# A hybrid decoder layer with a routed mixture of experts: expert work in units of 32 token rows instead of 64, on quarters of the TensorE array

## What is computed

```python
g_idx = jnp.argmax(group_logits, axis=-1)
e_logits = jnp.take_along_axis(all_logits, g_idx[:, None, None], axis=1)[:, 0]
top_vals, top_loc = lax.top_k(e_logits, TOP_K)                 # TOP_K = 2
expert_ids = g_idx[:, None] * EXPERTS_PER_GROUP + top_loc
...
def expert_block(args):
    xb, e = args                                               # w1, w3: [1024, 512], w2: [512, 1024]
    return (jax.nn.silu(xb @ w1[e]) * (xb @ w3[e])) @ w2[e]
```

```
32 30 35 4 19 24 25 81 | 7 33 82 50 39 34 26 15 | 25 60 105 78 45 57 23 91 | 7 57 41 63 48 38 51 75
59 24 17 36 35 77 26 130 | 12 9 11 5 13 4 12 12 | 18 19 7 17 16 23 9 9 | 0 8 4 1 3 6 14 12
```

## Time and profile before

| | |
|---|---|
| median of 3 runs | 2536.66 us |
| the profiled execution, its own time | 2528.26 us |
| its span on the core | 2526.5 us |
| first matmul of the first unit, end of the last one's | 1382.65 us, 2457.95 us |
| PE busy, DMA read from HBM | 1996.8 us (79%), 481.17 MB |

### The profile page before, as it was taken

One profiled execution on the slowest core, in us unless ns is written; L12 is line 12 of the kernel. 1 busy time (PEld: TensorE's weight loads), 2 busy tenths in 40 slices (PEclk: granted clock), 3 DMA queues, 4 the chain that ended last, 5 costly groups with the idle time before them and its releaser, 6 DMA issues.

```text
span 2526.5 us, 23324 instructions
## 1 busy us (share of the span) xinstructions
PE 1996.8 (79%) x7526; PEld 921.6 (36%) x7527; DVE 477.5 (19%) x919; ACT 272.2 (11%) x488; POOL 211.3 (8%) x318
## 2 busy tenths in 40 slices
PE   6345789689899999998971888888888888878770
PEld 5235544554444444443540232332323323222220
DVE  3534210420211111111233111101111011100005
ACT  3000210212000000000110000110010010100002
POOL 1480000000000000000003000000101000000002
PEclk9765699889899999999985999999999999998995
DMA  7020312000011111103132999999999989999985
GB/s 255 0 63 3 125 42 63 25 0 25 34 38 37 37 37 37 37 33 138 67 154 96 377 401 396 406 411 393 380 410 387 403 338 405 402 406 407 412 331 199
DMA packets 144850, 518.79 MB, mean 205 GB/s; under 512 B 29376, under 2 KB 66272, under 8 KB 127904
## 3 DMA queue, kind: packets, MB, share of 16 engines
q1 hardware_dynamic: 121952, 456.39, 47.0%
q0 software_dynamic: 9888, 38.08, 4.4%
q10 hardware_dynamic: 12976, 23.87, 2.6%
HBM read 481.17 MB, written 35.95 MB: 205 GB/s over the span
## 4 chain that ended last, share of the span: by engine, by line
PE 71%; DVE 11%; DMA 8%; POOL 3%; ACT 3%; issue 3%; SPq 1%; POOLq 0%; ACTq 0%; DVEq 0%
PE act_bank L656 22%; PE act_bank L911 18%; PE dve_bank L656 15%; PE act_bank L926 8%; DMA unit<-in_w 7%; DVE unit L1147 2%; DVE gain_a L1531 2%; PE dve_bank L903 2%; PE dve_bank L663 1%; SPq L441 1%; PE dve_bank L733 1%; PE dve_bank L809 1%; DVE rows_store L1536 1%; DVE gain_a L1534 1%; ACT gain_a L1084 1%
## 5 line engine op out<-in xcount | busy, mean ns | idle before, releaser
L656 PE MATMUL act_bank<-norm_store,unit 128*128 128x512 f32 x896 | 394.4, 594 | 8.7 <-DVE unit L1388 8.7
L911 PE MATMUL act_bank<-unit,gain_a 128*64 128x512 f32 x1504 | 345.6, 613 | 50.8 <-DVE gain_a L1531 33.8
L926 PE MATMUL act_bank<-unit,rows_store 128*64 128x512 f32 x1168 | 266.7, 597 | 51.6 <-DVE rows_store L1536 51.6
L656 PEld LDWEIGHTS act_bank<-norm_store,unit 128*128 128x128 f32 x896 | 170.8, 191 | 223.9 <-issue 223.9
L911 PE MATMUL act_bank<-mid_store,gain_a 128*64 128x512 f32 x832 | 187.4, 603 | 27.5 <-DVE gain_a L1531 19.9
L911 PEld LDWEIGHTS act_bank<-unit,gain_a 128*64 128x64 f32 x1504 | 110.3, 141 | 251.2 <-issue 233.1
L926 PEld LDWEIGHTS act_bank<-unit,rows_store 128*64 128x64 f32 x1168 | 92.2, 136 | 179.3 <-issue 178.5
L1534 DVE TENSOR_TENSOR gain_a<-gain_a,act_bank 128x256 f32<-128x256 f32 x73 | 30.8, 422 | 591.5 <-ACT gain_a L1084 583.8
L656 PE MATMUL dve_bank<-unit,mid_store 128*128 128x512 f32 x256 | 113.1, 601 | 8.9 <-DMA unit<-in_w_router 8.9
L1531 DVE COPY gain_a<-dve_bank 128x512 f32<-128x512 f32 x73 | 50.5, 692 | 360.7 <-PE dve_bank L903 360.7
L1400 DVE TENSOR_TENSOR rows_store<-dve_bank,rows_store 128x512 f32<-128x512 f32 x48 | 33.2, 692 | 440.8 <-PE dve_bank L656 440.8
(11 more groups left out here) (208 smaller groups left out, 1485.5 us busy)
## 6 DMA issues: line engine op xcount, KB each, us to landing
unit<-in_w SPq DMA_DIRECT2D x150, 2048.0 KB, 25.6
mid_store<-in_w SPq DMA_DIRECT2D x42, 2048.0 KB
unit<-in_w_gate SPq DMA_DIRECT2D x24, 512.0 KB, 5.2
unit<-in_w_in SPq DMA_DIRECT2D x4, 2048.0 KB, 12.7
unit_results<-unit POOLq DMA_DIRECT2D x4, 2048.0 KB, 16.2
unit_results<-lane_row ACTq DMA_DIRECT2D x52, 128.0 KB, 8.2
unit_results<-rows_store ACTq DMA_DIRECT2D x50, 128.0 KB
unit<-in_w_branch SPq DMA_DIRECT2D x24, 256.0 KB, 5.2
```

Of the source, the lines that this page charges most:

```text
L656: ins = nc.tensor.matmul(out_, stationary, moving, start=first and n == 0, stop=n == len(pairs) - 1)
L911: ins = nc.tensor.matmul(act_bank[0][h * CAP:(h + 1) * CAP, :].rearrange("t (w n) -> t w n", w=2), xT[:, k], w13[s][:, :, k, h * FF // 2:( ...
L926: ins = nc.tensor.matmul(act_bank[1 + s][z * CAP:(z + 1) * CAP, :], hidT[:, j, h * CAP:(h + 1) * CAP], w2s[s][:, n, z * HALF:(z + 1) * HAL ...
```

## The change

- `CAP`, the rows of a unit, goes from 64 to 32. A unit now uses the array in four quarters of 32 columns (`QUARTERS`). An up step has four matmuls of 256 columns (128 of w1, 128 of w3) where it had two of 512, and a down step four of 256 where it had two of 512. PSUM tiles, SiLU, product and copies have half the columns.
- Quarter h takes up columns h, h + 4, h + 8 and so on: the moving operand is read at a step of four floats. So after the transpose, partition p of `hidT` holds hidden columns 4p to 4p + 3, and the down matrix can be loaded as 4 consecutive rows per partition, in one run of 16 KB.
- There is one `xg` buffer, one gather in flight, and PE transposes the rows of unit u + 1 behind the up matmuls of unit u (`turn_tokens`), with DVE's copy to `xT` behind the copy to `hidT` (`take_tokens`). The program ends with one gather that fetches nothing.
- Slots of the table that hold no token point past the last row and are skipped by the gather (`bounds_check`). `xg` is cleared once.
- Results leave in four stores of 32 rows by 256 columns instead of two of 64 by 512.
- Every engine reads three numbers from `spans` per expert; PE and DVE read two before.
- The number of units per expert and the block of a token come from rounding, in place of comparisons with 15 steps.

```diff
-CAP = 64
+CAP = 32
+QUARTERS = P // CAP
...
-        xg = [rows_in[0], rows_in[1], rows_norm[0]]
-        xT = gain_a[:, 0:512].rearrange("p (k t) -> p k t", k=KD)
+        FQ, DQ = FF // QUARTERS, D // QUARTERS
+        xg = rows_in[0][0:CAP, :]
+        xT = gain_a[:, 0:256].rearrange("p (k t) -> p k t", k=KD)
...
             def expert_down(w_down, s):
-                sp.dma_start(w2s[s], w_down.rearrange("e (k p) n -> p (e k) n", p=P)).then_inc(down_loaded[s], 16)
+                sp.dma_start(w2s[s].rearrange("p k n -> p (k n)"), w_down.rearrange("e (p k) n -> p (e k) n", p=P)
+                             ).then_inc(down_loaded[s], 16)
...
-            def gather(c, s, u):
-
-                pool.wait_ge(per_slot["tok_turned"][s], c + 1)
...
+            def gather(c, s, u, t, column=None):
+
+                column = u if column is None else column
+                pool.wait_ge(tok_turned, u + 1)
                 pool.nop(nofuse=True)
...
+                pool.indirect_dma_start(xg, None, xf_dram,
+                                        bass.IndirectOffsetOnAxis(ap=gather_idx[:, 0:1], axis=0),
+                                        bounds_check=T - 1, oob_is_err=False).then_inc(tok_gathered, 16)
...
+            def work(c, s, u, t):
+
+                pe.wait_ge(xT_ready, u + 1)
 
                 pe.wait_ge(up_loaded[s], (t + 1) * UP_INC)
                 for k in range(KD):
-                    for h in range(2):
+                    for h in range(QUARTERS):
                         ins = nc.tensor.matmul(
-                            act_bank[0][h * CAP:(h + 1) * CAP, :].rearrange("t (w n) -> t w n", w=2), xT[:, k],
-                            w13[s][:, :, k, h * FF // 2:(h + 1) * FF // 2], start=k == 0, stop=k == KD - 1)
+                            act_bank[0][h * CAP:(h + 1) * CAP, 0:2 * FQ].rearrange("t (w n) -> t w n", w=2), xT[:, k],
+                            w13[s][:, :, k, h:FF:QUARTERS], start=k == 0, stop=k == KD - 1)
                 ins.then_inc(per_slot["gu_ready"][s], 1)
+                turn_tokens(u + 1)
 
                 pe.wait_ge(per_slot["hid_ready"][s], c + 1)
-                turn(dve_bank[1], [hid[:, j * P:(j + 1) * P] for j in range(2)]
-                     ).then_inc(per_slot["hid_turned"][s], 1)
+                turn(dve_bank[1], [hid]).then_inc(per_slot["hid_turned"][s], 1)
...
-                for n in range(4):
-                    h, j = n // 2, n % 2
-                    for z in range(2):
-                        ins = nc.tensor.matmul(act_bank[1 + s][z * CAP:(z + 1) * CAP, :],
-                                               hidT[:, j, h * CAP:(h + 1) * CAP],
-                                               w2s[s][:, n, z * HALF:(z + 1) * HALF], start=n == 0, stop=n == 3)
+                for j in range(QUARTERS):
+                    for z in range(QUARTERS):
+                        ins = nc.tensor.matmul(act_bank[1 + s][z * CAP:(z + 1) * CAP, 0:DQ], hidT[:, j],
+                                               w2s[s][:, j, z * DQ:(z + 1) * DQ], start=j == 0, stop=j == QUARTERS - 1)
...
-                act.wait_ge(per_slot["y_stored"][s], c * 32 + 32)
-                nc.scalar.activation(y_rows[s], act_bank[1 + s][:, :], ACT.Copy).then_inc(per_slot["y_drained"][s], 1)
+                act.wait_ge(per_slot["y_stored"][s], c * (16 * QUARTERS) + 16 * QUARTERS)
+                nc.scalar.activation(y_rows[s], act_bank[1 + s][:, 0:DQ], ACT.Copy).then_inc(per_slot["y_drained"][s], 1)
                 act.wait_ge(per_slot["y_drained"][s], c + 2)
-                for z in range(2):
-                    act.dma_start(y_dram[bass.ds(u * CAP, CAP), z * HALF:(z + 1) * HALF],
+                for z in range(QUARTERS):
+                    act.dma_start(y_dram[bass.ds(u * CAP, CAP), z * DQ:(z + 1) * DQ],
```

More of the change, by code:

```diff
@@ L148, in program @@
         spans = sb("spans", [1, 3, SLOTS * TURNS], I32)
-        unit_tokens = sb("unit_tokens", [CAP, UNITS], I32)
-        gather_idx = [sb(f"gather_idx{s}", [CAP, 1], I32) for s in range(SLOTS)]
+        unit_tokens = sb("unit_tokens", [CAP, UNITS + 1], I32)
+        gather_idx = sb("gather_idx", [CAP, 1], I32)
         nT = norm_store[:, :].rearrange("p (k t) -> p k t", k=KD)
@@ L223, in program @@
         exp_out = unit[9][:, 3264:3336]
-        cap_steps = small[:, 464:479]
         exp_in = small[:, 546:618]
@@ L228, in program @@
         square_dump = rows_norm[0][:, 0:HALF]
[L229 removed]
         w13 = [b[:, :].rearrange("p (w k n) -> p w k n", w=2, k=KD) for b in (pair[5], mid_store, pair[8])]
         w2s = [tiles(n, 4) for n in (7, 4, 10)]
[L234 to L239 removed]
+        FQ, DQ = FF // QUARTERS, D // QUARTERS
+        xg = rows_in[0][0:CAP, :]
+        xT = gain_a[:, 0:256].rearrange("p (k t) -> p k t", k=KD)
+        silu_g = gain_a[:, 256:384]
+        hid = gain_a[:, 384:512]
+        hidT = gain_a[:, 512:640].rearrange("p (j t) -> p j t", j=QUARTERS)
+        y_rows = [rows_norm[1][:, 0:DQ], lane_row[:, 0:DQ], spatialT[:, 0:2, :].rearrange("p h t -> p (h t)")]
         y_pick = [[unit[4 + 2 * s + c][:, 0:D] for c in range(2)] for s in range(2)]
@@ L262, in program @@
         spatial_loaded, spatial_masked = sem("spatial_loaded"), sem("spatial_masked")
-        idx_copied = [sem(f"idx_copied{s}") for s in range(SLOTS)]
+        idx_copied = sem("idx_copied")
+        tok_gathered, tok_turned, xT_ready = sem("tok_gathered"), sem("tok_turned"), sem("xT_ready")
         w_loaded = {n: sem(f"w_{n}_loaded") for n in
@@ L327, in one @@
                 end = eng.value_load(spans[0:1, 1, at], min_val=0, max_val=SLOT_UNITS)
-                if numbered:
-                    shift = eng.value_load(spans[0:1, 2, at], min_val=0, max_val=UNITS)
+                shift = eng.value_load(spans[0:1, 2, at], min_val=0, max_val=UNITS)
                 with eng.Fori(first, end) as c:
-                    if numbered:
-                        t = nc.s_assert_within(c + shift, 0, UNITS - 1, skip_runtime_bounds_check_because=(
-                            "the units of all experts are at most UNITS"))
-                    body(c, s, t)
+                    body(c, s, nc.s_assert_within(c + shift, 0, UNITS - 1, skip_runtime_bounds_check_because=(
+                        "the units of all experts are at most UNITS")), t)
             with eng.Fori(0, E // SLOTS) as t:
@@ L520, in _ @@
             nc.gpsimd.iota(token_id[:, :], [[P, NT]], base=0, channel_multiplier=1).then_inc(masks_made, 1)
-            step(nc.gpsimd.memset(unit_tokens[:, :], 0))
+            step(nc.gpsimd.memset(unit_tokens[:, :], T))
             pool.dma_start(table_rows, unit_tokens[:, :]).then_inc(table_cleared, 16)
@@ L593, in _ @@
                            allow_small_or_imprecise_dtypes=True).then_inc(masks_made, 1)
-            nc.gpsimd.iota(cap_steps, [[CAP, 15]], base=CAP, channel_multiplier=0,
-                           allow_small_or_imprecise_dtypes=True).then_inc(masks_made, 1)
+            for s in range(2):
+                pool.wait_ge(xf_stored[s], 16 * NT // 2)
+            pool.wait_ge(act_filled, jobs_end(act_jobs, "xfT"))
+            nc.gpsimd.memset(xg, 0.0).then_inc(tokens_cleared, 1)
             pool.wait_ge(routed, 1)
@@ L1485, in _ @@
             step(v.memset(n_units, 0.0))
-            over = cmp_store[:, 0:E * 15].rearrange("p (e k) -> p e k", k=15)
-            tt(over, bc(before[:, NT], 2, 15), bc(cap_steps, 1, E), ALU.is_gt)
-            step(v.tensor_reduce(n_units[:, 0:E], over, AX.X, ALU.add))
-            ts(n_units[:, 0:E], n_units[:, 0:E], 1.0, ALU.add)
+            ts(n_units[:, 0:E], before[:, NT], CAP / 2 - 0.5, ALU.add, 1.0 / CAP, ALU.mult)
+            ts(n_units[:, 0:E], n_units[:, 0:E], ROUND, ALU.add)
+            ts(n_units[:, 0:E], n_units[:, 0:E], ROUND, ALU.subtract, 1.0, ALU.max)
             for s in range(SLOTS):
@@ L1509, in _ @@
                 step(v.tensor_reduce(base[:, c], pick, AX.X, ALU.add))
-            over = cmp_store[:, 0:2 * NT * 15].rearrange("p (n k) -> p n k", k=15)
-            tt(over, bc(small[:, 128:144], 2, 15), bc(cap_steps, 1, 2 * NT), ALU.is_ge)
-            step(v.tensor_reduce(small[:, 160:176], over, AX.X, ALU.add))
+            ts(blk, pos, CAP / 2 - 0.5, ALU.subtract, 1.0 / CAP, ALU.mult)
+            ts(blk, blk, ROUND, ALU.add)
+            ts(blk, blk, ROUND, ALU.subtract)
             mac(res, blk, float(-CAP), pos)
-            mac(res, res, float(UNITS), base)
+            mac(res, res, float(UNITS + 1), base)
             tt(res, res, blk, ALU.add)
```

77 lines of the change are left out of this document (35 added, 42 removed).

## The result

The changed kernel takes **2691.66 us** (median of 4 runs, 2690.34 to 2692.71) against 2536.97 for the kernel before, a ratio of 1.062 [1.060, 1.064]: 6% slower. (One of the four runs of the kernel before took 4504.48 us; the ratio leaves it out.) The forecast was 2700 us. The profiled execution has a span of 2688.7 us, 162.2 more than before.

A forecast was written before the change was run, and what follows sets the result against it. PE's cycle was taken to bound the kernel up to expert 40, mostly the weights' stream after it. +184 us for the first phase, -21 for the second and 0 for routing give 2691, forecast 2700 us; range 2475 to 2800.

The forecast's parts named there:

- Up matmuls: PE's 16 groups of four matmuls per unit, operand read at a step of four floats: 7.6 us, 4.0 of it for the step.
- The value of DVE's norm: Alternative price of the step from DVE's strided norm, 0.78 ns more per column: 3.2 us per unit, up at 6.8.
- the upper one of 30 us: Bound for up if the four quarters' strided reads share one port, one after the other; as a rival 4900 us, chance 0.12.
- The cycle: PE's time per unit: up 7.6 plus 3.4 us to the end of down, 11.0 within an expert; 12.3 between, 1.3 sticking out.
- The side loops: Three loops beside PE's cycle (gather, stores, ACT): about 9, 10.7 and 10.5 us, all below 11.0 and 12.3, so hidden.
- loop (a): One gather in flight, from transposes through issue and landing to the next transposes: about 9 us, bounds 5.5 and 12.4.
- The weights' stream: DMA per expert of one unit: 15.75 us against a measured 16.7; long runs for the down matrix taken as 0.2.
- The sum: Experts 0 to 39 888 us against 704, the rest 350 against 371, routing 0: +163, 2691 profiled, 2700 as median.
- The step costs nothing: Rival: strided up takes 3.7 us, PE's cycle 7.1 and 8.4, side loops rule; 2560 us, range 2500 to 2620, chance 0.22.
- loop (b): A second unit of one expert waits until its predecessor's stores have landed: 10.7 us, bounds 8 and 16.
- Faster: Rival: step free, gather and stores land in some 7 us, weights bound everything; 2465 us, cycle below 8.7, chance 0.08.
- break-even of 9.5: Cycle per unit at which the changed kernel would equal the one before: (704 + 21) / 76 = 9.5 us.

## Why the prediction was right

The forecast was 2700 us and 2691.66 were measured. By its steps:

- **Up matmuls, 7.6 us.** Measured 7.49. The step's share, taken as 4.0 us from PE's own weight loads, is 7.49 - 3.66 = 3.83, and the 0.1 for twice the instructions is about the 3.66 - 3.54 that four quarters take over the rate of two halves. The value of DVE's norm, 3.2, was too small. That the two rows, both of a step of eight, hold for four is shown by the runs at four and eight (7.49 and 7.62). The lower bound of nothing fell with the run without a step, and the upper one of 30 us with the changed kernel's own 7.49; the halves, where a stream pays the same, leave no sharing at all.
- **The cycle, 11.0 within and 12.3 between experts.** Measured 10.84 and 12.37. The rest behind the up matmuls was 3.4 and is 3.35; transposes and copy cost nothing, as said. The share of the loop end that sticks out was taken as 1.3 us, with 0.5 and 2 as bounds; the timeline has an idle time of 1.75, and the difference between the two medians is 1.5.
- **The side loops stay hidden.** They do: in the first phase ACT waited for its own stores twice (4.9 and 4.5 us), PE for no gather after the first. That the clock stays at full speed was not said, but the sum needs it: it does, 1.00 throughout. The landing of a gather is 6.8 us by the median, where 8.9 was the row of before and about 7.2 went into the 9 us of loop (a).
- **The weights' stream, 15.75 us per expert.** Measured 46.91 and 47.07 us for three experts, 15.7. Against 16.7 before that is 1.0 less, of which the long runs gave 0.24 (taken: 0.2). The whole second phase, from SiLU to SiLU, is 23 us shorter than before, and the runs split it: 8 us with units of 64 and no empty rows fetched, 9 more with units of 32, whose stores are half as large, and 6 more with the long runs. What in these parts is gathers and what stores was not tried.
- **The sum.** 890 for 888 in the first phase, 346 for 350 in the second, +0.8 for 0 elsewhere: +162 for +163. The nearness in the first phase is in part luck: by the means, 12.49 between experts is 8 us more over 40 units than 12.3, and 10.85 within them 5 us less over 36 than 11.0. The forecast's other 8 us are the 0.3% between profile and median that I added: after the change the median lies only 0.9 us above the profiled execution's own time, 2690.72 us.

Where it was wrong is in the rivals, which the runs without a step let me measure. (The first one's 2560 us is also the sum without the share of the median that it names; with it, it is some 2568.)

- *The step costs nothing* was given 2560 us, with 757 us for the first phase from "about 9.2 between experts, 10.8 within". Measured 2516.8 and 716. PE's own cycle was right: 7.0 and 8.55 for 7.1 and 8.4. The cycle between experts is 10.0, more than taken, and that within an expert 7.7, much less. Between experts it took too little: in the first phase PE waits 31 us for gathers and 37 us for the product that comes late by way of ACT, and TensorE's clock, which the rival puts at full speed without saying so, was at 0.90 and cost 58 us. Within an expert the step that failed is loop (b): "copy 0.5, three issues of 0.66 before the last one, landing 8.2, so 10.7". ACT's timeline in the run without a step has two results of one expert in the same buffer:

```profile
1712.70 0.38 ACT L1089 ACTIVATE lane_row<-act_bank 128x256 f32<-128x256 f32 x1 [3.36 <-PE act_bank L927]
1713.27 1.76 ACTq L1092 DMA_DIRECT2D unit_results<-lane_row  x4
...
1719.73 0.38 ACT L1089 ACTIVATE lane_row<-act_bank 128x256 f32<-128x256 f32 x1 [3.39 <-PE act_bank L927]
```

  Copy follows copy after 7.03 us, and the second waits for PE and not for the stores. The four issues take 1.76 us in all, so the last begins 1.4 us after the first, and its store had landed 1719.73 - 1713.27 - 1.4 = 5.1 us later at the latest, where the row of the kernel before, with stores four times as large (128 KB, now 32), gave 8.2. Taken was a loop of 10.7 us that binds each time; here it was 7.03 without binding, and in the first phase it bound 7 times.
- *Faster* had its point of decision at a cycle of 8.7 us. Without a step the mean cycle is 716 / 76 = 9.4, close to the break-even of 9.5 that the prediction named, and the kernel is 0.65% faster than before. PE's own cycle is 594 / 76 = 7.8, below the point of decision; it is the waits and the clock that keep the measured one above it.
- The better version was not among the rivals: the cycle of 64 rows shortened by what the change brings beside the quarters. Its expectation of 2465 to 2485 was too low. It let the weights rule throughout, at 16.0 us per expert. Measured is a mixture: experts of several units run on PE's cycle, those of one unit on the weights, and the slow up groups behind the waits come on top.

So two parts of the change pay: the early transposes with one gather and no empty rows, some 29 us together, and the longer runs, 6. The quarters by themselves lose about 16 of these (2516.8 against 2500.6, each against its own runs of the kernel before: 0.9935 and 0.988). It is not that 76 short cycles are too long in sum: undisturbed they are 36 x 7.0 + 40 x 8.55 = 594 us, and 49 of 12.60 are 617. But on top of these come 122 us of waits and low clock with quarters, and 62 with units of 64, so that the first phase is 37 us longer; the second is 9 us shorter. The step of four, with the longer runs that it allows, loses 175.

## What to carry to other kernels

Price a strided moving operand by the 16-byte pieces that it touches: with float32 a step of two costs 4% on TensorE, and a step of four doubles the time of the matmul, so that a layout made for longer DMA runs has to pay for itself out of what these give, here only 0.24 us per 2 MiB. Smaller units halve the column times and not the cycle (12.6 us became 7.0 and 8.55), and with the shorter cycle PE waits more often and then also runs at the lower clock. Before cutting them, take the steps off the path that stay the same for every unit. And look at the second engine's share in the windows: of 1.8 us cut from PE's cycle 0.5 arrived, and the rest went to waits for weights and to the slow matmuls behind them.

## What the runs showed of the hardware

- **The price of a piece of 16 bytes** is some 1.86 ns for TensorE's moving operand, whether two or four quarters read at once, and next to nothing (4%) as long as two floats of a piece are used. The forecast had guessed the size, and not that it is this even.
- **Four column quarters run side by side in full**: 16 groups of 256 columns in 3.66 us, 0.89 ns per column time, for 0.865 with two halves.
- **The clock after a strided stretch.** In the run with halves and a step of four, the same 16 down matmuls, contiguous in both, took 3.65 us in some units and 5.35 in others. The windows over exactly these stretches, and over the strided up matmuls behind the slow ones:

```profile
1630.08:1633.73 3.65, 3.65 (x17) 1.30 (x18) 0.00 (x0) 0.00 (x0) 0.00 (x0) 1.00 0.91 377
1695.62:1700.97 5.35, 5.34 (x17) 1.83 (x18) 0.00 (x0) 0.00 (x0) 0.00 (x0) 0.68 0.93 389
1702.49:1717.09 14.60, 14.60 (x32) 2.55 (x32) 0.00 (x0) 1.28 (x1) 0.92 (x1) 1.00 0.68 260
```

  The granted clock, behind the busy times, is 1.00 in the fast one and 0.68 in the slow one, 0.68 x 5.35 = 3.64: part of that stretch ran at 1.2 GHz, part at 2.4. Before both PE had been busy 14.6 us with strided matmuls, without a pause by the record. In the changed kernel the windows of the first phase show 1.00, and 1.93 us for down. Why the clock falls in one and not in the other was not tried.
- **The clock behind waits.** In the runs without a step, on quarters and on halves, the slow groups stand behind idle times of PE, as the 2.43 and 6.38 us above. In the run on quarters some have only pauses of about a microsecond before them. In the first phase the slow groups cost 58 us with quarters, 16 with units of 64, and nothing in the kernel before and in the changed kernel, whose granted clock is 1.00 there. No run changes the clock alone.
